# Hybrid decoder step on 8 cores: gates computed on 18 rows and spread through DRAM, w_down in eleven pieces, other places for the output tiles, and the last tile finished in halves

## The reference, cut to what matters

```
mod = silu(c) @ w_ada + b_ada      # c: one row per sequence; six vectors of 1024 each
h   = RMSNorm(x) * (1 + scale1) + shift1
mix = [pool mixer | gated short conv](h @ w_in)
x   = x + gate1 * RMSNorm(mix @ w_out)
h2  = RMSNorm(x) * (1 + scale2) + shift2
u   = dwconv3_causal(h2 @ ffn_w_up);  [a | b] = u
x   = x + gate2 * RMSNorm((silu(a) * b) @ ffn_w_down)
```

## Time and profile before

| | |
|---|---|
| runs (us) | 775.28, 776.26, 776.65; median 776.26 |
| the profiled execution | 774.03, its slowest core's span 772.5 |
| spans of the cores | 764.2 to 772.5 |
| PE busy on that core | 697.8 (90%) |
| DVE, ACT, POOL busy | 502.4, 346.7, 210.0 |
| first down projection begins, second begins, last matmul ends (chain of waits) | 440.43, 678.62, 764.22 |

### The profile page before, as it was taken

The page is one execution under the profiler, slowest core; times in us unless marked ns, Lnnn a source line. Parts: engine busy times, 40 slices in busy tenths (PEclk is TensorE's granted clock), DMA queues, the critical chain, the costliest instruction groups (busy, mean ns, idle before and its releaser), DMA issues.

```text
span 772.5 us, 12026 instructions; the slowest of 8 cores (764.2 to 772.5 us)
## 1 busy us (share of the span) xinstructions
PE 697.8 (90%) x4020; PEld 339.9 (44%) x4096; DVE 502.4 (65%) x660; ACT 346.7 (45%) x617; POOL 210.0 (27%) x252
## 2 busy tenths in 40 slices
PE   0269879998998999899998999999999999999995
PEld 0234445454544444345443444444444444444442
DVE  1247847788887898878975722228888888833222
ACT  2236725464647878673443421125455454521111
POOL 4202100001100222253443410005667667540000
PEclk9979989999999999999999999999999999999999
DMA  8999995288834876569499923334543444013211
GB/s 157 209 196 248 191 201 75 81 194 163 191 109 141 167 194 144 133 155 174 72 158 168 173 71 109 109 110 109 81 74 67 71 73 77 1 41 137 109 68 41
DMA packets 29293, 97.37 MB, mean 126 GB/s; under 512 B 4160, under 2 KB 4672, under 8 KB 28592
## 3 DMA queue, kind: packets, MB, share of 16 engines
q0 software_dynamic: 16272, 54.96, 42.1%
q1 hardware_dynamic: 12960, 41.65, 16.0%
HBM read 125.51 MB, written 18.92 MB: 187 GB/s over the span
## 4 chain that ended last, share of the span: by engine, by line
PE 73%; DMA 14%; DVE 4%; issue 4%; ACT 3%; POOL 1%; DVEq 0%; ACTq 0%; POOLq 0%
PE ps L796 44%; PE ps L298 21%; PE ps L289 5%; DMA arena<-w_ada 5%; DMA arena<-w_in_p 5%; DMA arena<-w_up 3%; PE ps L763 2%; PE ps L306 1%; ACT arena L714 1%; POOL arena L536 1%; ACT arena L555 1%; DVE arena L952 1%; DVE arena L1187 0%; DVE arena L988 0%; DVE arena L841 0%
## 5 line engine op out<-in xcount | busy, mean ns | idle before, releaser
L796 PE MATMUL ps<-arena 128*128 128x512 bf16 (+1 forms) x2347 | 436.2, 344 | 18.0 <-DMA arena<-w_in_p 5.8
L796 PEld LDWEIGHTS ps<-arena 128*128 128x128 bf16 x2400 | 201.1, 98 | 243.0 <-issue 25.8
L298 PE MATMUL ps<-arena 128*128 128x512 bf16 (+1 forms) x734 | 161.2, 380 | 0.7
L1187 DVE SCALAR_TENSOR_TENSOR arena<-ps,arena 128x1023 f32<-128x1023 f32 x88 | 112.6, 1279 | 42.9 <-ACT arena L1185 42.9
L1201 POOL TENSOR_TENSOR arena<-arena 128x1024 bf16<-128x1024 f32 x44 | 103.5, 2353 | 98.6 <-DVE arena L1191 52.9
L1191 DVE SCALAR_TENSOR_TENSOR arena<-ps,arena 128x1022 f32<-128x1022 f32 x88 | 112.8, 1282 | 9.5 <-DVE arena L1187 0.5
L298 PEld LDWEIGHTS ps<-arena 128*128 128x128 bf16 (+1 forms) x748 | 73.6, 99 | 88.0 <-issue 0.4
L562 DVE RECIPROCAL arena<-arena 128x1 f32<-128x1 f32 (+1 forms) x68 | 10.8, 159 | 135.5 <-ACT arena L557 132.3
L555 ACT ACTIVATE arena<-ps 128x1024 f32<-128x1024 f32 (+1 forms) x34 | 34.8, 1023 | 140.9 <-PE ps L298 127.5
L1185 ACT ACTIVATE arena<-ps,arena 128x1024 f32<-128x1024 f32 x88 | 97.5, 1108 | 0.0
L289 PE MATMUL ps<-arena 128*128 128x512 bf16 (+1 forms) x279 | 66.6, 379 | 2.7 <-DVE arena L562 1.3
(11 more groups left out here) (86 smaller groups left out, 412.9 us busy)
## 6 DMA issues: line engine op xcount, KB each, us to landing
arena<-w_up POOLq DMA_DIRECT2D x44, 512.0 KB, 6.7
y<-arena SPq DMA_DIRECT2D x32, 512.0 KB, 2.7
arena<-w_ada POOLq DMA_DIRECT2D x24, 512.0 KB, 12.9
arena<-x SPq DMA_DIRECT2D x22, 512.0 KB, 8.2
arena<-y SPq DMA_DIRECT2D x16, 512.0 KB, 3.5
arena<-x POOLq DMA_DIRECT2D x10, 512.0 KB, 26.4
arena<-w_down POOLq DMA_DIRECT2D x3, 1536.0 KB, 25.9
arena<-w_in_j POOLq DMA_DIRECT2D x4, 768.0 KB, 39.9
```

What stands on the lines that cost most here:

```text
L298: inst = e.matmul(out_ap, lhs_list[i], rhs_list[i], start=(first and i == 0), stop=(last and i == n - 1))
L796: inst = e.matmul(o_, l_, r_, start=st, stop=sp_)
L1187: K.op("dve", lambda e: e.scalar_tensor_tensor(tv[:, 1:1024], psv[:, 0:1023], fw_of(1, c), tv[:, 1:1024], ALU.mult, ALU.add), reads=rp + [ ...
```

## The change

1. **Gates on 18 rows.** The stationary operand is silu(c) itself (18 columns), so a piece is 8 matmuls that give 18 rows, with one pair of DVE operations. After the fourth piece the 18x1024 result is written to a DRAM scratch (`scr2`, `scr5`) and read back spread over the token rows: row 0 to 128 partitions, and four DMAs of 16 rows for the samples. These six DMAs are on SP's queue. The bias and norm rows are loaded into 18 partitions only. `REP` is gone.
2. **Places.** Gate 1's pieces 2 and 3 stand at n = 7. Gate 2's weights are loaded after pair 2, into space of `GT_` that is not yet in use, and its pieces run after pairs 4 to 7. Tiles 12 to 15 follow chunks 4, 7, 10, 13 (before: 4, 6, 8, 10), and the transposes of the last four tiles chunks 16 to 19 (before: 13 to 16).
3. **w_down in eleven pieces** of two pairs each, one after each of pairs 8 to 18 (before: four pieces, of 6, 6, 6 and 4 pairs, after pairs 13, 14, 16 and 18).
4. **The last tile.** Tile 16 of the down projection runs all its matmuls for one half of the columns, then for the other (before: the halves alternate in three cuts), and each half has its own square sum, product and store.

```diff
@@ gate_piece @@
-            for (M, m0, n0) in ((128, 0, 0), (TS, 128, 256)):
-                for kc in range(KC):
-                    inst = e.matmul(PS[0:M, bank, n0:n0 + 256], REP[:, kc, m0:m0 + M], wt[:, kc, :],
-                                    start=(kc == 0), stop=(kc == KC - 1))
...
+        K.op("pe", mm_group(PS[0:18, bank, 0:256], [SC[:, kc, :] for kc in range(KC)], [wt[:, kc, :] for kc in range(KC)]),
+             reads=[r_wt, r_sc], writes=[r_ps[bank]])
+        chain(K, "dve", [lambda e: e.tensor_tensor(G18[:, sl], PS[0:18, bank, 0:256], rowb[0:18, sl], ALU.add),
+                         lambda e: e.tensor_tensor(G18[:, sl], G18[:, sl], rowg[0:18, sl], ALU.mult)],
+              [r_ps[bank], r_rows], [r_g18])
+        if p == 3:
+            scr = dout("scr%d" % vec, [18, D])
+            r_scr = R("scr%d" % vec)
+            out_ops.append(dma1("sp", scr, G18, reads=[r_g18], writes=[r_scr]))
+            K.dma("sp", lambda e: [e.dma_start(out=dstP, in_=scr[0:1, :].to_broadcast([128, D]))] +
+                  [e.dma_start(out=dstS[r:TS:DS, :], in_=scr[1:1 + NS, :]) for r in range(DS)], next_misc(), 1 + DS,
+                  reads=[r_scr], writes=[r_dst])
@@ hook0 @@
-        if k in (4, 6, 8, 10):
-            t = 10 + k // 2
+        if k in (4, 7, 10, 13):
+            t = 12 + (k - 4) // 3
             o_tile(t, next_pair())
             b2(t)
-        if k in (13, 14, 15, 16):
-            h2_T(3, k - 13, 6 + k % 2, "act")
+        if k in (16, 17, 18, 19):
+            h2_T(3, k - 16, 6 + k % 2, "act")
...
-        if 9 <= i < 13:
-            gate2[i - 9]()
-        if i in (13, 14, 16, 18):
...
+        if 4 <= i < 8:
+            gate2[i - 4]()
...
+        if 8 <= i < 19:
+            load_wdn(i - 8)
@@ down_a, last_b @@
+        steps = [(n, hb) for n in range(3) for hb in range(2)] if t < 16 else [(n, hb) for hb in range(2) for n in range(3)]
...
+        for hb in range(2):
+            sq = K.op("act", lambda e, hb=hb: e.activation(out=JUNK[0:rows, :], in_=ps[hb], func=AF.Square, accum_out=ss[hb]),
+                 reads=[r_ps[b + hb]], writes=[r_ss[hb], r_junk])
+            K.op("dve", lambda e, hb=hb: e.tensor_tensor(tm[hb], ps[hb], GTS[0:rows, hb * 512:(hb + 1) * 512], ALU.mult),
+                 reads=[r_ps[b + hb], r_gt], writes=[r_lt[hb]], deps=[sq])
...
+        for hb in range(2):
+            K.op("dve", lambda e, hb=hb: e.scalar_tensor_tensor(xx[hb], tm[hb], rs, xx[hb], ALU.mult, ALU.add),
+                 reads=[r_lrs, r_lt[hb]], writes=[r_lx[hb]])
+            out_ops.append(dma1("sp", y_d[r0:r0 + rows, hb * 512:(hb + 1) * 512], xx[hb], reads=[r_lx[hb]]))
```

More of the change, by code:

```diff
@@ L374, in build_program @@
     SC = alloc([128, KC, 18], BF16)
-    REP = alloc([128, KC, 192], BF16)
+    G18 = alloc([18, D], F32)
     G1T = alloc([128, KC, 17], F32)
@@ L1059, in build_program @@
             PWS_item()
-        if n == 6:
-            for p in range(4):
+        if n in (6, 7):
+            for p in (2 * (n - 6), 2 * (n - 6) + 1):
                 gate1[p]()
@@ L1120, in build_program @@
     r_stfp = [R("stfp%d" % ch) for ch in range(NCH)]
-    r_wdnq = [R("wdn%d" % q) for q in range(4)]
-    s_wdnq = [new_sem("wdnq%d" % q) for q in range(4)]
-    def p1y():
-        for rr in r_wdnq + [r_stf, r_rows2] + r_stfp + r_pada[0:4]:
-            rr.alias(r_wout + [r for c in range(4) for r in r_by[c]] + r_bys + [r_gt1] + r_xn2)
+    r_wdn = [R("wdn%d" % q) for q in range(NPAIR // 2)]
+    r_pg2 = [R("pg2_%d" % p) for p in range(4)]
+    p1y = ([(WOUT, r_wout), (BY[0], r_by[0] + r_by[3]), (BY[1], r_by[1]), (BYS, r_bys), (GT1P, [r_gt1]), (GT1S, [r_gt1])] +
+           [(ap, [rr]) for ap, rr in zip(XN2, r_xn2)])
     def load_wdn(q):
-        i0, i1 = q * 6, min(NPAIR, (q + 1) * 6)
-        dma1("pool", flat(WDN[:, i0:i1, :]), wdn_d[:, i0 * D:i1 * D], writes=[r_wdnq[q]], sem=s_wdnq[q])
+        lo = place[id(WDN)][0] + q * 4 * D
+        r_wdn[q].alias(overlap(lo, lo + 4 * D, p1y))
+        dma1("pool", flat(WDN[:, 2 * q:2 * q + 2, :]), wdn_d[:, 2 * q * D:(2 * q + 2) * D], writes=[r_wdn[q]])
     def fw_of(kk, c):
@@ L1318, in down_a @@
         cuts = [0, NPAIR // 2, NPAIR - 1, NPAIR]
-        for n in range(3):
+        steps = [(n, hb) for n in range(3) for hb in range(2)] if t < 16 else [(n, hb) for hb in range(2) for n in range(3)]
+        for n, hb in steps:
             i0, i1 = cuts[n], cuts[n + 1]
             rg = r_gs[i0 // 2:(i1 + 1) // 2] if t == 16 else r_g[i0:i1]
-            for hb in range(2):
-                K.op("pe", mm_part(PS[0:rows, b + hb, :], [GT_[:, i, g0:g0 + rows] for i in range(i0, i1)],
-                                   [WDN[:, i, hb * 512:(hb + 1) * 512] for i in range(i0, i1)], n == 0, n == 2),
-                     reads=rg + (r_wdnq[0:2] if n == 0 else r_wdnq[2:4]), writes=[r_ps[b + hb]])
+            K.op("pe", mm_part(PS[0:rows, b + hb, :], [GT_[:, i, g0:g0 + rows] for i in range(i0, i1)],
+                               [WDN[:, i, hb * 512:(hb + 1) * 512] for i in range(i0, i1)], n == 0, n == 2),
+                 reads=rg + r_wdn[i0 // 2:(i1 + 1) // 2], writes=[r_ps[b + hb]])
@@ L1326, in down_a, with last_b @@
         tok[t] = (b, load_x(t, y_d, reads=[r_yd[t]]))
+    def last_b(t, b, xi):
+        r0, rows = tile_rows(t)
+        ps = [PS[0:rows, b + hb, :] for hb in range(2)]
+        tm = [TMP[0:rows, hb * 512:(hb + 1) * 512] for hb in range(2)]
+        xx = [XT[xi][0:rows, hb * 512:(hb + 1) * 512] for hb in range(2)]
+        ss = [STAT[0:rows, k, 17 + hb:18 + hb] for k, hb in ((ST_SSF, 0), (ST_SSF, 1))]
+        bb, rs = STAT[0:rows, ST_RSF, 17:18], STAT[0:rows, ST_RSF, t:t + 1]
+        r_ss = [R("lss%d" % hb) for hb in range(2)]
+        r_bb, r_lrs = R("lbb"), R("lrs")
+        r_lt = [R("lt%d" % hb) for hb in range(2)]
+        r_lx = [R("lx%d" % hb) for hb in range(2)]
+        for hb in range(2):
+            r_lt[hb].alias([r_tmp])
+            r_lx[hb].w = r_xt[xi].w
+            sq = K.op("act", lambda e, hb=hb: e.activation(out=JUNK[0:rows, :], in_=ps[hb], func=AF.Square, accum_out=ss[hb]),
+                 reads=[r_ps[b + hb]], writes=[r_ss[hb], r_junk])
+            K.op("dve", lambda e, hb=hb: e.tensor_tensor(tm[hb], ps[hb], GTS[0:rows, hb * 512:(hb + 1) * 512], ALU.mult),
+                 reads=[r_ps[b + hb], r_gt], writes=[r_lt[hb]], deps=[sq])
+            if hb == 0:
+                K.op("dve", lambda e: e.tensor_scalar(bb, ss[0], 1.0 / D, EPS, ALU.mult, ALU.add), reads=[r_ss[0]], writes=[r_bb])
+        K.op("act", lambda e: e.activation(out=rs, in_=ss[1], func=AF.Sqrt, bias=bb, scale=1.0 / D), reads=[r_ss[1], r_bb], writes=[r_lrs])
+        K.op("dve", lambda e: e.reciprocal(rs, rs), reads=[r_lrs], writes=[r_lrs])
+        for hb in range(2):
+            K.op("dve", lambda e, hb=hb: e.scalar_tensor_tensor(xx[hb], tm[hb], rs, xx[hb], ALU.mult, ALU.add),
+                 reads=[r_lrs, r_lt[hb]], writes=[r_lx[hb]])
+            out_ops.append(dma1("sp", y_d[r0:r0 + rows, hb * 512:(hb + 1) * 512], xx[hb], reads=[r_lx[hb]]))
```

62 lines of the change are left out of this document (33 added, 29 removed).

## The result

Median of 7 runs 758.66 us (758.05 at the least), the kernel before beside it 775.28; the ratio is 0.9781, 95% interval 0.9768 to 0.9794: **faster, by 16.6 us**. In some executions of most kernels, two of these seven among them, the cores of one die or of both have a lower granted clock; those are left out of all ratios and means here. Predicted were 757 us, and a gain of 19.3. A second measurement of the same kernel on another chip gave 0.9801 (0.9758 to 0.9845).

A forecast was written before the change was run, and what follows sets the result against it. PE was taken as full from 112 to 170 us, with gains possible where it idles or its clock is low. Terms sum to 19.3 off 774.03, giving 754.7; the median runs 2.2 above, so 757, range 751 to 765.

The forecast's parts named there:

- The wait before gate 1: Stage 1: fewer bytes ahead of gate 1's weights let piece 1 end at 106.1 to 107.1; -4.5 us, bounds -3.0 and -7.
- gate 1's pieces: Stage 1, pieces 2 and 3: 0.93 us each instead of 1.86, in a stretch where PE is full; -1.9 us.
- the gain of stage 1 is given back: Rival, stage 1: loads of gate 1's successors wait for ring buffers that PE frees; 763 us, chance 0.12.
- Gate 1 through DRAM: Store and reads before L953: 8 to 9 us, under the 10.7 available; 0 us.
- a sign of being wrong: First use of gate 1: the prediction is wrong if L953 waits for a DMA.
- The same trip for gate 2: Gate 2's DRAM trip starts after pair 7, its result first used behind pair 21; 0 us.
- Output tiles: Pair stage, 280 to 325 us: new places cut idle PE from 6.1 to 1 to 4; -3.5 us, bounds +0.5 and -6.1.
- forecast lag of DVE: Among the tiles, with three chunks per tile: DVE some 14.5 us per period against PE's 13.8, so DVE stays longer.
- Gate 2's pieces: Pair stage: four pieces of 1.86 us become four of 0.93; -3.7 us, lost if DVE bounds that stretch.
- w_down in eleven pieces: Pair stage: w_up lands in 6 to 10 us, removing its late load and low clock; -4.7 us, bounds 0 and -4.7.
- smaller loads: Rival, pair stage: 512 KB pieces cost more per byte, 8.9 us per pair, w_up stays late; 762 to 765, chance 0.07.
- The last tile: End of the kernel: finishing in halves shortens the last operations from 4.46 to 3.5 us; -1.0 us, bounds -0.4 and -1.4.

The follow-up runs named there:

- e5: Changed kernel with gate 1's bias and norm rows loaded to 128 partitions again, 18 used; no ratio (two runs), mean core -9.6 us against the kernel before.
- e12: The changed kernel measured again without an edit, on another chip; 760.21 us, ratio 0.980 to the kernel before.
- e2: Changed kernel with output tiles 12 to 15 and the last transposes at their old places; ratio 0.985 to the kernel before.
- e3: Kernel before with only the gates changed to 18 rows through DRAM, at their old places; ratio 0.994 to the kernel before.
- e1: Changed kernel with w_down in the four old pieces after pairs 13, 14, 16 and 18; ratio 0.981 to the kernel before.
- e8: Changed kernel with four further unused 512 KB loads after pair 8, w_down still in eleven pieces; ratio 0.986 to the kernel before.

## Why the prediction was right, point by point

The time was right within 2 us, but of a sum of 19.3 us some terms were too large, one was put down to the wrong part of the change, and one was too small. By the traces of all cores the change gave 5.3 in stage 1 (forecast 6.4), 9.3 between there and the down projection (11.9) and 2.4 at the end (1.0): 17.0. That the errors partly cancel, and that the total came out this near, is luck.

- **The wait before gate 1 (4.5) and gate 1's pieces (1.9).** The mechanism was right: piece 1 ended at 106.1, in the forecast 106.1 to 107.1, and with the bytes back the mean of the cores went from 105.7 or 106.5 to 109.8 (e5). When it reached its first output tile, core 6 was 6.4 us ahead (matmuls at 125.87 in place of 132.27), the sum of the two terms; that is the luck of the core, for the eight range from 2.3 to 7.9, and the mean is 5.5, in all traces with either stage 1 some 4.7. Over the whole of stage 1 the mean of the cores was 5.3 ahead, in the second measurement 3.3, and 4.1 if all traces with either code are taken (seven and two): from 112 to 170 PE now has 3.5 us without work where it had 0.7, `w_ada` loads near 167 among them, and the transposes that wait for L716 are new. That is the rival "the gain of stage 1 is given back", in part. The wait before gate 1 was one of 2.9, not two of 4 in all.
- **Gate 1 through DRAM (0).** Right in size, but with less room than forecast. The trip took 8.8 us on core 6 (6.6 to 9.5 over the cores), and L953 started 9.6 us after the gate's last operation, not 10.7. So on core 7 L953 did wait for a read (0.3 us), and on three cores in e12 0.8 to 1.0 us. The prediction named such a wait as a sign of being wrong; it is one of DVE, of 1 us at most, and whether PE felt it is not shown. The same trip for gate 2, also priced at 0 because its result is used late, was seen too narrowly: what stands behind it on SP is what nearly costs (e5: 3.4 us).
- **Output tiles (3.5).** Right in size by e2 (3.2 to 3.5), not by the way forecast. Between the two kernels the stretch gained 2.5 (2.1 idle, 0.4 low clock); e2 gives more, since there gate 2's pieces stand in it as well, with a low clock that the kernel before hardly had. Idle PE fell from 5.9 to 3.8, inside the 1 to 4 that were forecast; the wait before the transpose did not go but changed hands, from L988 (2.0) to L763 (1.7). The 2.54 for L988 in the working is not what that operation costs: it ran beside POOL's product (295.36 to 297.71), and takes 0.75 alone. The places took it out of the product's way (0.75 for the last three tiles on core 6), and gate 2's L763 got into it. The forecast lag of DVE, 14.5 against PE's 13.8, also counts the wait of 0.81 for ACT that the same sentence lets be filled; without it DVE has 13.7 and no lag.
- **Gate 2's pieces (3.7).** Right in size: of the 9.3 between stage 1 and the down projection 2.5 are the tiles', 3.0 the late `w_up` with its low clock, and 3.7 are left. Where the pieces stood, e3 shows that it would have turned into waits.
- **w_down in eleven pieces (4.7).** The effect came, the step failed. With the four old pieces a late `w_up` hardly came back and the low clock not at all (0.5 us, e1). With four more loads among eleven pieces both came (5.8 us, e8), but elsewhere. The prediction read the 18.7 us landings as the fault of the pieces next to them; e1 has landings of 17.0 and waits 1.1 at most. What it missed is when the pieces go out: before the change the first stood behind gate 2, whose space it takes, and left 1.1 us ahead of the second; with gate 2 early it leaves 7.0 ahead (e1). That this order is what made `w_up` late is argued from the two traces, not run by itself. The four `w_ada` loads were through by then (landings of 5.0 to 6.2 us ahead of the first piece). The landings with eleven pieces came as forecast, 5.0 to 12.7 us over the cores; the 8.9 us per pair in the rival "smaller loads" stand in no row.
- **The last tile (1.0).** The mechanism was right, the term too small: 2.4. The chain of operations took 3.04, not 3.5, and the last store carries half the bytes and lands 2.7 us after DVE's end in place of 3.7, which the sum had left out.
